# A two-block transformer kernel on one core: the norms' root moved behind the projections, and the transposes that feed them done block by block

## What is computed

```python
h = rmsnorm(x, g);  proj = h @ w_in          # 2048 -> 6144 (+8), block 1;  7168 (+16), block 2
o = two kinds of attention (block 1) or two recurrences (block 2), normed per head
x = x + o @ w_out                            # 2048 -> 2048
h2 = rmsnorm(x, g)
x = x + relu(h2 @ w_up)**2 @ w_down          # block 1: 8192 wide; block 2: PEER, router and 16384 experts
x = rmsnorm(x, g_final)                      # after each block
# rmsnorm(x, g) = x * rsqrt(mean(x*x) + 1e-6) * g
```

## Time and profile before

| | us |
|---|---|
| runs | 3787.45, 3794.88, 3795.14 (median 3794.88) |
| profiled execution: span, first to last instruction | 3783.5 (the page gives no other time of it) |
| PE busy | 3487.8 (92%) |
| DVE busy | 2050.4 (54%) |
| ACT busy | 1460.2 (39%) |
| products of chunks, L234 to L236 | 5109.7 summed, since they overlap |

### The profile page before, as it was taken

How to read it: one execution, slowest core, us unless ns; L and a number is a source line. 1 busy time by engine, 2 the same in 40 slices (tenths; PEclk the granted TensorE clock), 3 DMA queues, 4 the chain that set the end, 5 groups by cost and what they waited for, 6 DMA issues and landing times.

```text
span 3783.5 us, 41166 instructions
## 1 busy us (share of the span) xinstructions
PE 3487.8 (92%) x15882; PEld 2837.2 (75%) x15882; DVE 2050.4 (54%) x2111; ACT 1460.2 (39%) x1219; POOL 211.5 (6%) x292
## 2 busy tenths in 40 slices
PE   7998889999999799965889848999999999999998
PEld 6887778888888678853767736888888888888886
DVE  4443545555555553356454997555555555555555
ACT  4335444343434433333234335333333333333333
POOL 0000000000000000021700043000000000000000
PEclk9997999999999899976989979999999999999999
DMA  6551345555555455500024426555555555555553
GB/s 252 184 186 45 109 149 188 178 184 182 188 177 187 146 178 188 178 0 1 1 90 167 156 67 194 189 198 193 198 199 192 196 191 197 192 196 189 199 194 123
DMA packets 119360, 607.43 MB, mean 161 GB/s; under 512 B 11504, under 2 KB 44528, under 8 KB 49776
## 3 DMA queue, kind: packets, MB, share of 16 engines
q1 hardware_dynamic: 81632, 571.73, 42.8%
q10 hardware_dynamic: 37648, 34.61, 3.0%
HBM read 587.42 MB, written 18.87 MB: 160 GB/s over the span
## 4 chain that ended last, share of the span: by engine, by line
PE 44%; DVE 6%; issue 1%; ACT 1%; DMA 0%; POOL 0%; DVEq 0%; POOLq 0%; ACTq 0%
PE pj L234 13%; PE pj L235 13%; PE pj L236 13%; DVE hotA L1510 1%; DVE lo L223 1%; PE pt L297 1%; PE pj L1178 1%; DVE hotB L1514 0%; DVE idx L1433 0%; PE pm L1554 0%; DVE pos L1433 0%; DVE vals L1431 0%; PE pt L1194 0%; PE pj L1194 0%; DVE best L1431 0%
## 5 line engine op out<-in xcount | busy, mean ns | idle before, releaser
L223 DVE TENSOR_TENSOR lo<-raw,hi 128x2048 fp32r<-128x2048 f32 x536 | 1227.5, 2291 | 1247.7 <-ACT hi L219 1246.9
L219 ACT ACTIVATE hi<-raw 128x2048 fp32r<-128x2048 f32 x536 | 1022.2, 1914 | 1337.7 <-PE pj L236 1319.1
L234 PE MATMUL pj<-hi,xh 128*128 128x512 f32 x2752 | 1094.3, 398 | 4.6 <-DVE lo L223 4.6
L235 PE MATMUL pj<-lo,xh 128*128 128x512 f32 x2752 | 1093.0, 397 | 0.0
L236 PE MATMUL pj<-hi,xl 128*128 128x512 f32 x2752 | 1092.3, 397 | 0.0
L234 PEld LDWEIGHTS pj<-hi,xh 128*128 128x128 f32 x2752 | 519.5, 189 | 131.3 <-DVE lo L223 5.5
L236 PEld LDWEIGHTS pj<-hi,xl 128*128 128x128 f32 x2752 | 519.5, 189 | 126.9
L235 PEld LDWEIGHTS pj<-lo,xh 128*128 128x128 f32 x2752 | 519.2, 189 | 125.6
L234 PE MATMUL pj<-hi,coef_h 128*128 128x512 f32 x1536 | 612.5, 399 | 0.0
L236 PE MATMUL pj<-hi,coef_l 128*128 128x512 f32 x1536 | 609.0, 396 | 0.0
L235 PE MATMUL pj<-lo,coef_h 128*128 128x512 f32 x1536 | 608.6, 396 | 0.0
(11 more groups left out here) (335 smaller groups left out, 1888.2 us busy)
## 6 DMA issues: line engine op xcount, KB each, us to landing
raw<-w_peer SPq DMA_DIRECT2D x256, 1024.0 KB, 4.8
raw<-w_mlp SPq DMA_DIRECT2D x128, 1024.0 KB, 4.8
raw<-w_in SPq DMA_DIRECT2D x104, 1024.0 KB, 4.9
raw<-w_out SPq DMA_DIRECT2D x32, 1024.0 KB, 4.8
raw<-w_q SPq DMA_DIRECT2D x16, 1024.0 KB, 4.9
gates_scratch<-stage ACTq DMA_DIRECT2D x8, 2048.0 KB, 8.9
gate_e<-gates_scratch ACTq DMA_DIRECT2D x32, 512.0 KB, 3.3
resid<-x SPq DMA_DIRECT2D x2, 1024.0 KB, 6.1
```

The lines of the kernel that those rows point to most:

```text
L219: nc.scalar.activation(hi[:, j, :], raw[:, j, :], ACT.Copy).then_inc(hi_ready, 1)
L223: nc.vector.tensor_tensor(lo[:, j, :], raw[:, j, :], hi[:, j, :].bitcast(F32), ALU.subtract).then_inc(lo_ready, 1)
L234: nc.tensor.matmul(pair[:, t, :], sh[:, k0 + k, tok], hi[:, j, cols], start=begin, stop=False)
L235: nc.tensor.matmul(pair[:, t, :], sh[:, k0 + k, tok], lo[:, j, cols], start=False, stop=False)
```

## The change

1. The norm's factor `rstd` is no longer multiplied into the stationary operand. Transposes read the raw `resid` (L469's `src`), `xh` and `xl` carry only the gain, and `rstd` is applied per token where a projection leaves PSUM: by the `scale` of ACT's copies and of Relu and Gelu (each split in two, one for each token tile), and by DVE for the narrow tails. At the join of MLP and IN2 the gain is the product of both norms' gains (`gain2`), and the factor the product of both roots; `resid` itself is still scaled, now during IN2.
2. The station is cut into four lifts (`lift_pe`, `lift_act`, `lift_dve`: one block b each, bodies as in the station). Lifts 0 to 2 are issued among the last chunks of OUT1, MLP and OUT2, lift 3 after the next stage's first chunk. Squares, variance and root are issued among the next stage's first chunks.
3. At the start, `x` comes in four blocks of 512 columns in turns with the first four weight chunks, behind the identity and `small`. Lifts 0 and 1 go ahead of chunk 0, lift 2 after it, lift 3 after chunk 1.
4. At the end, squares are made for each block of 512 columns once it is added, into `last_sq` and `part_ss`, and DVE sums them.
5. In `ffn_act` and `ffn_dve` the hook `step(j)` stands ahead of `make_hi` and `make_lo`, where it stood behind.

WQ's hooks on DVE and PE, and MLP's on DVE, mirror those shown. Left out too: the tails, new semaphores, and `column`, `head_gain` and `both_gains`, which give the gain's column.

```diff
+        def wide_act(act, q0, groups, evac, out, rs, before=None, late=False, between=None):
+
+            def evacuate(i, g):
+                act.wait_ge(pe_used, (i * 2 + (q0 + g)) * SLOTS + SLOTS)
+                for t in range(TT):
+                    ins = nc.scalar.activation(out[:, t, bass.ds((i * 2 + g) * NB, NB)], pj[g][:, t, :], ACT.Copy,
+                                               scale=stat[:, rs + t:rs + t + 1])
+                ins.then_inc(evac, 1)
+
             def body(i):
                 for g in range(2):
                     for j in range(SLOTS):
+                        if before and isinstance(i, int):
+                            before(g, j)
+                        if late and isinstance(i, int) and g == 1 and j == 2:
+                            evacuate(0, 0)
                         make_hi(act, *next_ones(i * 2 + (q0 + g), j))
-                    if out is not None:
-                        act.wait_ge(pe_used, (i * 2 + (q0 + g)) * SLOTS + SLOTS)
-                        nc.scalar.activation(out[:, :, bass.ds((i * 2 + g) * NB, NB)], pj[g][:, :, :],
-                                             ACT.Copy).then_inc(evac, 1)
+                    if not (late and isinstance(i, int) and g == 0):
+                        evacuate(i, g)
...
+        def out_pe(pe, q0, evac, n):
+            for g in range(4):
+                if g >= 2:
+                    pe.wait_ge(evac, g - 1)
+                for j in range(SLOTS):
+                    if g == 0:
+                        pe.wait_ge(tp_l, 4 * n + j + 1)
+                    multiply(pe, q0 + g, j, pj[g % 2], xh, xl, 4 * j, j == 0, j == SLOTS - 1)
+                    if g == 3 and j >= 1:
+                        lift_pe(pe, n + 1, j - 1, resid, evac, j)
+
+        def out_act(act, q0, n, gain):
+            for g in range(4):
+                for j in range(SLOTS):
+                    make_hi(act, *next_ones(q0 + g, j))
+                    if g == 3 and j >= 2:
+                        lift_act(act, n + 1, j - 2, gain, (q0 + 3) * SLOTS + j - 1)
+
+        def out_dve(dve, q0, evac, n, gain):
+            for g in range(4):
+                for j in range(SLOTS):
+                    make_lo(dve, *next_ones(q0 + g, j))
+                    if g == 3 and j >= 2:
+                        lift_dve(dve, n + 1, j - 2, gain)
+                dve.wait_ge(pe_used, (q0 + g) * SLOTS + SLOTS)
+                part = resid[:, :, g * NB:(g + 1) * NB]
+                nc.vector.tensor_tensor(part, part, pj[g % 2][:, :, :], ALU.add).then_inc(evac, 1)
...
+                    if last and after:
+                        after(n)
...
-                nc.scalar.activation(hid[:, :, :], pair[:, :, :], func).then_inc(S["up_evac"], 1)
+                for t in range(TT):
+                    ins = nc.scalar.activation(hid[:, t, :], pair[:, t, :], func, scale=stat[:, 6 + t:7 + t])
+                ins.then_inc(S["up_evac"], 1)
...
-                make_hi(act, *next_ones(q0, j))
                 if step:
                     step(j)
+                make_hi(act, *next_ones(q0, j))
...
+        def squares_act(act, n, t, ready=None):
+            if ready:
+                act.wait_ge(*ready)
+            nc.scalar.activation(nat[:, t, :], resid[:, t, :], ACT.Square, accum_out=stat[:, t:t + 1]).then_inc(nm_sq, 1)
+
+        def root_act(act, n):
             act.wait_ge(nm_var, n + 1)
             nc.scalar.activation(stat[:, 4:6], stat[:, 2:4], ACT.Sqrt).then_inc(nm_sd, 1)
...
+        def lift_pe(pe, n, b, src, ready=None, value=0):
+            if ready is not None:
+                pe.wait_ge(ready, value)
+            if b >= 2:
+                pe.wait_ge(tp_l, 4 * n + b - 1)
+            for k in range(4):
+                for t in range(TT):
+                    col = (4 * b + k) * P
+                    at = (k % 2) * 256 + t * P
+                    tr = nc.tensor.transpose(st_ps[b % 2][:, k // 2, at:at + P], src[:, t, col:col + P], ident)
+            tr.then_inc(tp, 1)
+
+        def lift_act(act, n, b, gain, free=None):
+            act.wait_ge(tp, 4 * n + b + 1)
+            if free is not None:
+                act.wait_ge(pe_used, free)
+            for k in range(4):
+                ins = nc.scalar.activation(xh[:, 4 * b + k, :], st_ps[b % 2][:, k // 2, (k % 2) * 256:(k % 2) * 256 + 256],
+                                           ACT.Copy, scale=gain(4 * b + k))
+            ins.then_inc(tp_h, 1)
+
+        def lift_dve(dve, n, b, gain):
+            dve.wait_ge(tp_h, 4 * n + b + 1)
+            for k in range(4):
+                ins = nc.vector.scalar_tensor_tensor(
+                    xl[:, 4 * b + k, :], st_ps[b % 2][:, k // 2, (k % 2) * 256:(k % 2) * 256 + 256],
+                    gain(4 * b + k), xh[:, 4 * b + k, :].bitcast(F32),
+                    ALU.mult, ALU.subtract)
+            ins.then_inc(tp_l, 1)
...
         def query_act(act):
             for g in range(4):
                 for j in range(SLOTS):
+                    if g == 0 and j < 2:
+                        lift_act(act, 5, j + 2, column(S_GFFN), (Q_OUT2 + 3) * SLOTS + j + 3)
                     make_hi(act, *next_ones(Q_WQ + g, j))
+                    if g == 0 and j >= 2:
+                        squares_act(act, 4, j - 2, (out2_evac, 4))
                     router_act(act, g - 1, j)
+                if g == 0:
+                    root_act(act, 4)
+                    act.wait_ge(nm_rs, 5)
                 act.wait_ge(pe_used, (Q_WQ + g) * SLOTS + SLOTS)
-                nc.scalar.activation(qn[:, :, g * NB:(g + 1) * NB], pj[g % 2][:, :, :], ACT.Copy).then_inc(wq_evac, 1)
+                for t in range(TT):
+                    ins = nc.scalar.activation(qn[:, t, g * NB:(g + 1) * NB], pj[g % 2][:, t, :], ACT.Copy, scale=stat[:, 6 + t:7 + t])
+                ins.then_inc(wq_evac, 1)
...
+            sp.dma_start(cst[:, 0:1, :], cst_d[:, 0:1, :]).then_inc(s_first, 16)
+            sp.dma_start(small[:, :], small_d).then_inc(s_first, 16)
+            x_block(0)
+            x_block(1)
+            first_chunk(0)
+            x_block(2)
+            first_chunk(1)
+            x_block(3)
+            first_chunk(2)
+            first_chunk(3)
             sp.dma_start(wtail[:, :, 0:8], wf_d).then_inc(wt_loaded, 16)
+            sp.dma_start(cst[:, 1:N_CONST, :], cst_d[:, 1:N_CONST, :]).then_inc(s_const, 16)
             sp.dma_start(att[:, :, :], att_d).then_inc(s_att, 16)
             sp.dma_start(gfin[:, :], gfin1_d.broadcast_to([P, D])).then_inc(gfin_in, 16)
-            stream(w_in_d, Q_IN1, G1)
+            stream(w_in_d, Q_IN1, G1, 1)
...
+            act.wait_ge(s_first, 32)
+            lift_act(act, 0, 0, column(S_GATTN))
+            lift_act(act, 0, 1, column(S_GATTN))
             make_hi(act, 0, 0, first=True)
-            station_act(act, 0, lambda k: S_GATTN + k)
-            for j in range(1, AHEAD):
-                make_hi(act, 0, j, first=True)
-            tail_act(act, 0, 8)
-            wide_act(act, Q_IN1, G1, in1_evac, proj1)
+            lift_act(act, 0, 2, column(S_GATTN))
+            make_hi(act, 0, 1, first=True)
+            lift_act(act, 0, 3, column(S_GATTN))
+            make_hi(act, 0, 2, first=True)
+
+            def before_in1(g, j):
+                if g == 0 and j in (1, 2):
+                    squares_act(act, 0, j - 1, (s_x[3], 16))
+                if g == 0 and j == 3:
+                    root_act(act, 0)
+                    tail_act(act, 0, 8)
+                if g == 1 and j == 0:
+                    act.wait_ge(nm_rs, 1)
+            wide_act(act, Q_IN1, G1, in1_evac, proj1, 6, before_in1, late=True)
...
+            def before_mlp(j):
+                if j < 2:
+                    lift_act(act, 2, j + 2, column(S_GMLP), (Q_OUT1 + 3) * SLOTS + j + 3)
+                if j >= 2:
+                    squares_act(act, 1, j - 2, (out1_evac, 4))
+                if j == 3:
+                    root_act(act, 1)
+                    act.wait_ge(nm_rs, 2)
+
+            def after_mlp(j):
+                if j >= 2:
+                    lift_act(act, 3, j - 2, both_gains, (Q_MLP + 2 * MLP_SB - 2) * SLOTS)
+            ffn_act(act, Q_MLP, MLP_SB, ffn_sems["mlp"], ACT.Relu, True, Q_END, before_mlp, None, after_mlp)
+
+            def before_in2(g, j):
+                if g == 0 and j < 2:
+                    lift_act(act, 3, j + 2, both_gains)
+                if g == 0 and j >= 2:
+                    squares_act(act, 2, j - 2, (ffn_sems["mlp"]["dn_evac"], 4 * MLP_SB))
+                if g == 0 and j == 3:
+                    root_act(act, 2)
+                if g == 1 and j == 1:
+                    squares_act(act, 3, 0, (nm_out, 4))
+                    squares_act(act, 3, 1)
+                    act.dma_start(lb[:, :, :], lbl_d.broadcast_to([P, 2, H * P])).then_inc(lbl_in, 16)
+                    tail_act(act, 1, 16)
+                    root_act(act, 3)
+                if g == 1 and j == 2:
```

(100 more changed lines are left out.)

190 lines of the change are left out of this document (76 added, 114 removed).

## The result

The changed kernel takes 3732.19 us, the median of 4 runs (3731.47 to 3739.92), against 3793.85 for the kernel before beside it: a ratio of 0.9842 [0.9828, 0.9856], 61.7 us less. The mechanisms of the forecast took place, with small errors in their sizes; some 16 of the missed microseconds came from something no step had.

A forecast was written before the change was run, and what follows sets the result against it. PE was taken as the bound, busy 92% of the span, with gaps at norms, start and end. Terms +5.1 - 12.1 - 22.6 + 0.3 - 12.1 + 0.5 - 2.4 = -43.3 us, from 3794.9 to 3751.6; range 3738 to 3770.

The forecast's parts named there:

- The sum of -43.3: Whole kernel: start, three joins, HGRN bound, evacuations and end together save 43.3 us; chance 0.58.
- Joins: Three norms inside the kernel: gaps of 15.6, 26.13 and 15.6 us shrink to 3.5 each, gaining 12.1, 22.6 and 12.1.
- The slack of 11 us: At the joins: ACT and DVE have operands ready 11 us before PE's chunks need them.
- The bound's +0.3: HGRN bound, where PE already waits 1.85 us: DVE's work there comes 0.3 us later; bounds 0 and 5.4.
- Split evacuations: Two half copies cost 0.17 us more, showing once at MLP's first `hid`; tails 0.15 twice; together +0.5 us.
- The end: After the last add: fewer squares remain before the table load and first scaling; gain 2.4 us, bounds 2.0 to 2.8.
- The start: First chunks: queue order idles PE 5.95 us twice, clock falls, chunk 3 at 52.9 against 47.85; +5.1 us.
- Runs lie 4.0 to 11.6 above the span: Baseline choice: runs exceed the profiled span of 3783.5 us, median by 11.4, so the sum starts from 3794.9.
- clock held: Rival, start: the clock stays up in the two pauses, so the start costs 0.4 us; 3747, chance 0.13.
- late lifts: Rival, joins: each keeps one pause of 5.95 us with 2.3 of clock, +25 us; 3776, chance 0.15.
- slower: Rival, long projections: removed gaps were rest, so granted clock drops; 150 us of it give 3819, chance 0.03.
- The start keeps what chunk 0 gains: Rival, start: chunk 0's 14 us gain persists, -14 instead of +5.1; 3733, chance 0.07.

The follow-up runs named there:

- Runs 2: Kernel before with 192 unused bytes a partition ahead of the narrow weights, putting the stationary tiles where the changed kernel has them; 3779.70 us, ratio 0.9959.
- run 3: Changed kernel with 832 unused bytes a partition, bringing the stationary tiles back to the old placement modulo 1024; 3750.77 us, ratio 0.9878.
- run 7: Changed kernel with chunks 0, 1, 2 split ahead of lifts 1, 2, 3 and ACT's table load ahead of its first wait; 3714.43 us, ratio 0.9790.
- `p_four`: Kernel of run 7 with all stationary tiles at placement 64 and `lo` moved by 64 too; 3715.17 us, one execution.

## Why the prediction was wrong

**The step that failed** is a term that the sum put at nothing without a reason. Its terms are joins, evacuations, end and start; the chunks themselves, "5.62 us a chunk, 0.234 a product, 536 chunks", were read from the trace of before and taken to stay. The new and longer tiles (`gain2`, `part_ss`, `stat`, `small`) have no term. They moved the stationary tiles by 192 bytes against the weights, and every product came 1.0 ns sooner behind the last. Runs 2 and 3 show it from both sides: 15.7 us gained with nothing else, 16.0 given back with all else kept. The spacing accounts for 12.6 of it; the rest of some 3 us lies elsewhere, is no more than unedited stages wander, and wasn't taken apart. What remains of the 19.4 is 1.3 to 1.7 by which the edits gave more than 43.3, 1.0 by which the kernel before was quicker than its earlier median, and about 1 of spread.

**The sum of -43.3 held.** At equal placement it is -44.6 at 0, -45.0 at 192 and -44.7 at 160. Read stage by stage from the traces at placement 0 (kernel before, run 3): start +5.6, OUT1 to IN2 -34.9, third join -11.1, end -2.5, together -42.9. That it agrees within 2 us is partly luck, since unedited stages wander by more. By its terms:
- Joins, 3.5 us left of each: a lift costs 0.79 at the join and 0.86 in a stream, so 3.4. No product waits there. The slack of 11 us counted on three engines was enough. OUT1, MLP and IN2 with their two joins lost 34.9 us in the traces at placement 0 (forecast 12.1 + 22.6, less 0.3). From OUT2 to the first expert chunks 11.1 are gone (409.5 to 398.4), forecast 12.1.
- The bound's +0.3: 2.16 against 1.85. The scaling of `resid` had been caught up by then.
- Split evacuations: the first `hid` is waited for 0.24 us longer (product start to start 2.60 against 2.36), +0.17 forecast. The tails' share was not read.
- The end: 2.47, forecast 2.4. The root again starts 1.30 us after its table load does; nothing of the further drain of the Trainium skill's "ScalarE: Activation LUTs", section "What ACT_TABLE_LOAD costs", is to be seen, and by its figure the gain would have been 1.0 us.
- The start: +6.4, forecast +5.1. The pauses are 5.88 us (5.95), ended by `lo`, twice. The clock fell in both: it is 0.50 around the first products behind each (30 to 33 and 45 to 48 us), as "TensorE: Matmul & The Clock Gate" of the Trainium skill, Part 1, would have it. Chunk 0 was 1.35 us late: ACT's table load used to run while `x` was under way, and now stands behind ACT's first wait, 1.28 us at 8.16. The count had missed it, and it went the other way than the miss. Chunk 3 of the kernel before starts at 47.61; the prediction's 47.85 is 0.24 late.
- The bounds of the terms reach 3765, not 3761, once the 5.4 us at the bound are counted; the range was wide enough for that at its upper end and had nothing for placement at its lower one.
- "Runs lie 4.0 to 11.6 above the span": taking the median of the runs and not the span was right. The profiled execution had a quick pass through the recurrences, 7 us under nearly half of the other traces. Spans alone (3783.5 to 3738.1) would give 45.4 us for the change, where the medians have 61.7: the quick pass would have hidden the miss.

**The rivals.** Neither "clock held" (3747) nor "late lifts" (3776) nor "slower" occurred: the last sixteen slices have a clock of 9 as before. "The start keeps what chunk 0 gains", 3733, had the measured time and not the mechanism: chunk 3 was later, not 14 us sooner. Only the stage table and the placement runs tell these two apart. That the rival became true in run 7 (chunk 3 at 35.9, 11.7 sooner than before) shows that its condition, the order on three queues, was the right one.

**What stays open.** Why placement sets the spacing. The runs show a dependence on the relative place of moving and stationary tile with quick places at 96 and above all at 160, slow ones at 0, 256, 512 and 1024 (5.62 us a chunk), 5.60 at 128, 192 and 224, and 5.58 at 32. Whether 160 is the quickest, and whether it is a conflict in SBUF's reads or something else, no run tells; `p_four` shows that a product's own distance is not all. The single-run placements rest on one trace each. The 337 to 344 us of the recurrences were not traced to a cause either.

## What to carry to other kernels

Before summing a change's instructions, list what it does to addresses: a kernel whose time is 12,864 equal products pays or earns 13 us for each nanosecond of their spacing, and a pad of a few bytes tests it without touching the schedule; compare versions at equal placement. Take the norm's root and other per-token factors out of the way of a matmul stage first (34.5 us of gaps here), and interleave its transposes second (11 to 15). At a start, every engine's program order counts: put the work of the chunk that is due ahead of the work for the one after it, and force table loads ahead of the first wait.

## What the runs showed of the hardware

- Product spacing (128x512, fp32r, full granted clock) of 234.3, 233.3 or 226.8 ns by the relative placement of the operands in SBUF: 94.5 us of 3795 for the kernel before, from 160 bytes of padding.
- The fastest version run here is kernel 7 at 160: 3637.10 us (3634.70 to 3639.71), 158.0 less than the kernel before beside it (3795.06). 94.5 of them the kernel before gets from padding alone, more than from the whole change.
- A pause of 5.88 us ends with products 0.43 us apart instead of 0.23, for 4.7 us at 32.14.
